# Encoder layer on one core: the first FFN product with 512-column matmuls, its partial products chained in three PSUM banks

## The reference, cut to what matters

```python
h = h + rmsnorm(mix, g_post_mix)
gu = rmsnorm(h, g_pre_ffn) @ w_ffn_in        # (512, 2048) @ (2048, 11264)
g, u = jnp.split(gu, 2, axis=-1)
h = h + rmsnorm((jax.nn.silu(g) * u) @ w_ffn_out, g_post_ffn)
```

## Time and profile before

| | us |
|---|---|
| median of 3 runs | 2728.7 (2728.43 to 2729.52) |
| the profiled execution, its own time | 2728.66 |
| its span, first to last instruction | 2726.5 |
| granted TensorE clock, mean | 0.998 |
| TensorE busy in matmuls | 2694.1 |
| VectorE busy | 1946.7 |
| ScalarE busy | 1086.7 |

### The profile page before, as it was taken

The page is one execution under the profiler, slowest core; times in us unless marked ns, Lnnn a source line. Parts: engine busy times, 40 slices in busy tenths (PEclk is TensorE's granted clock), DMA queues, the critical chain, the costliest instruction groups (busy, mean ns, idle before and its releaser), DMA issues.

```text
span 2726.5 us, 41873 instructions
## 1 busy us (share of the span) xinstructions
PE 2694.1 (99%) x16358; PEld 2416.1 (89%) x16358; DVE 1946.7 (71%) x2269; ACT 1086.7 (40%) x1413; POOL 338.1 (12%) x205
## 2 busy tenths in 40 slices
PE   8999999999999999999999999999999999999997
PEld 7999888888888888878999999999999888888886
DVE  7888655555554432276999999999998888886524
ACT  7333333333334422253444444444444444444422
POOL 0000000000000000000244344343433000000000
PEclk9999999999999999999999999999999999999999
DMA  6433522222225544253444434344346755544322
GB/s 257 155 117 117 150 91 77 77 82 88 77 89 152 148 152 146 94 187 121 171 144 146 154 142 167 133 155 164 123 173 258 259 187 183 214 167 153 139 93 108
DMA packets 174237, 396.15 MB, mean 145 GB/s; under 512 B 17846, under 2 KB 52014, under 8 KB 171566
## 3 DMA queue, kind: packets, MB, share of 16 engines
q1 hardware_dynamic: 149120, 340.99, 36.6%
q10 hardware_dynamic: 25006, 53.60, 5.1%
HBM read 336.81 MB, written 57.73 MB: 145 GB/s over the span
## 4 chain that ended last, share of the span: by engine, by line
PE 85%; issue 10%; DMA 1%; DVE 1%; ACT 1%; SPq 0%; POOL 0%; DVEq 0%; POOLq 0%
PE bank L2339 10%; PE bank L2337 10%; PE bank L2338 10%; PE bank L2178 8%; PE bank L2179 8%; PE bank L2180 8%; PE bank L2417 5%; PE bank L2418 5%; PE bank L2419 5%; PE bank L2586 4%; PE bank L2588 4%; PE bank L2589 4%; PE bank L2211 1%; DMA x_f<-xT 1%; DMA o_a_first<-w_ffn_pieces 0%
## 5 line engine op out<-in xcount | busy, mean ns | idle before, releaser
L2337 PE MATMUL bank<-act_hi,w_hi 128*128 128x256 f32 x1664 | 471.2, 283 | 2.4 <-DVE act_lo L1449 1.4
L2338 PE MATMUL bank<-act_lo,w_hi 128*128 128x256 f32 x1664 | 470.9, 283 | 0.0
L2339 PE MATMUL bank<-act_hi,w_lo 128*128 128x256 f32 x1664 | 470.9, 283 | 0.0
L844 ACT CAST w_hi<-w_raw 128x1024 fp32r<-128x1024 f32 x210 | 211.7, 1050 | 585.3 <-PE bank L2180 326.6
L1358 DVE TENSOR_TENSOR w_lo<-w_raw,w_hi 128x1024 fp32r<-128x1024 f32 x208 | 246.5, 1222 | 244.3 <-ACT w_hi L844 244.3
L2337 PEld LDWEIGHTS bank<-act_hi,w_hi 128*128 128x128 f32 x1664 | 319.4, 192 | 2.9 <-DVE act_lo L1449 1.6
L2338 PEld LDWEIGHTS bank<-act_lo,w_hi 128*128 128x128 f32 x1664 | 319.5, 192 | 0.1
L2339 PEld LDWEIGHTS bank<-act_hi,w_lo 128*128 128x128 f32 x1664 | 319.5, 192 | 0.0
L2178 PE MATMUL bank<-act_hi,w_hi 128*128 128x512 f32 x752 | 296.2, 394 | 0.3 <-DVE w_lo L1358 0.3
L2179 PE MATMUL bank<-act_lo,w_hi 128*128 128x512 f32 x752 | 293.1, 390 | 0.0
L2180 PE MATMUL bank<-act_hi,w_lo 128*128 128x512 f32 x752 | 293.0, 390 | 0.0
(11 more groups left out here) (293 smaller groups left out, 5952.5 us busy)
## 6 DMA issues: line engine op xcount, KB each, us to landing
w_raw<-w_in SPq DMA_DIRECT2D x92, 512.0 KB, 4.0
w_a_even<-w_ffn_in SPq DMA_DIRECT2D x80, 512.0 KB, 4.3
xop<-xop_dram SPq DMA_DIRECT2D x35, 1024.0 KB, 11.5
w_a_odd<-w_ffn_in SPq DMA_DIRECT2D x60, 512.0 KB, 4.7
xop_dram<-h_sums ACTq DMA_DIRECT2D x20, 1024.0 KB, 6.4
o_a_odd<-w_ffn_pieces SPq DMA_DIRECT2D x40, 512.0 KB, 7.7
o_a_even<-w_ffn_pieces SPq DMA_DIRECT2D x39, 512.0 KB, 6.9
w_raw<-w_ffn_in SPq DMA_DIRECT2D x36, 512.0 KB, 5.2
```

What stands on the lines that cost most here:

```text
L2337: nc.tensor.matmul(out, w_hi[:, slot, k], hi, start=k == 0, stop=False)
L2338: nc.tensor.matmul(out, w_hi[:, slot, k], lo, start=False, stop=False)
L2339: last = nc.tensor.matmul(out, w_lo[:, slot, k], hi, start=False, stop=k == HALF - 1)
```

## The change

- A product of the first FFN stage is 8 times two matmuls: the high weight against high and low activation side by side (512 columns, two runs of 256 in `act_both` for P0, P3, P5, P6, one run in `d1`, `t2`, `d2`), and the low weight against the high activation (256 columns, added to the first half of the same bank). The two halves of a bank are added when it is read.
- The products of a pair go into three banks: a takes P0 and P3, g takes P1 and P5, b takes a copy of P0, then P2, P4 and P6. Even pairs use banks 0, 1, 5, odd pairs 2, 3, 4.
- ScalarE makes six copies per pair (`keep_chain`) in place of one; before P2, P4 and P6 PE waits for one of them (`kept`).
- VectorE's additions become six, one pair's last ones at the start of the next pair (`finish_up`, `finish_hidden`). All four sums of weight blocks stay on VectorE; they move ahead of the low part of their step, and the fourth moves from step 6 to step 0 of the next pair (`ffn_fourth`).
- Silu, the high parts of the hidden tiles, GpSimd's low part of the sums and their stores move to later steps. The banks of the second product and of the tail are renumbered. The landing semaphores of `xop` are grouped as (0), (1, 2), (3, 4), (5, 6) in place of (0, 1), (2, 3), (4, 5), (6).

The core of the diff:

```diff
+PAIR_BANKS = ((0, 1, 5), (2, 3, 4))
+PAIR_CHAIN = (0, 1, 2, 0, 2, 1, 2)
-CHAINS = (((2, 3), (4, 5), (6, 7)), ((0, 1), (4, 5), (2, 3)), ((6, 7), (4, 5), (0, 1)))
+CHAINS = (((0, 1), (2, 5), (6, 7)), ((3, 4), (2, 5), (0, 1)), ((6, 7), (2, 5), (3, 4)))
...
-        xop_landed = [sem(f"xop_landed{j}") for j in (0, 2, 4, 6)]
+        xop_landed = [sem(f"xop_landed{j}") for j in (0, 1, 3, 5)]
...
             def operands(i, first=False):
+                if not first:
+                    low_of_sums(i + (-1))
                 pool.wait_ge(hid_ready, i * 2 + (CH + 1))
...
-                pool.wait_ge(h_summed, i * SUMS + SUMS)
-                pool.wait_ge(h_hi_ready, i * 3 + 3)
-                low_in_place(h_sums, slice(0, 4))
...
+            def keep_chain(n, q, j, first):
+                a, g, b = PAIR_BANKS[q % 2]
+                if j == 0:
+                    if not first:
+                        act.wait_ge(combined, n * COPIES + (COMBINED_FFN - COPIES))
+                    nc.scalar.copy(bank[:, b], bank[:, a]).then_inc(kept, 1)
+                elif j == 1:
+                    if not first:
+                        act.wait_ge(combined, n * COPIES + (COMBINED_FFN - COPIES + 2))
+                    nc.scalar.copy(second_kept[:].rearrange("p a t -> p (a t)"), bank[:, g]).then_inc(kept, 1)
+                elif j == 2:
+                    if not first:
+                        act.wait_ge(combined, n * COPIES + (COMBINED_FFN - COPIES + 5))
+                    nc.scalar.copy(third_kept[:].rearrange("p a t -> p (a t)"), bank[:, b]).then_inc(kept, 1)
+                elif j == 3:
+                    act.wait_ge(combined, n * COPIES + COMBINED_FFN)
+                    nc.scalar.copy(low_half[:], bank[:, a, S:]).then_inc(kept, 1)
+                elif j == 4:
+                    act.wait_ge(hid_ready, n + CH)
+                    nc.scalar.copy(up_kept[:].rearrange("p a t -> p (a t)"), bank[:, b]).then_inc(kept, 1)
+                elif j == 6:
+                    act.wait_ge(combined, n * COPIES + (COMBINED_FFN + 1))
+                    nc.scalar.copy(low_half[:], bank[:, b, S:]).then_inc(kept, 1)
...
                         act.wait_ge(op_done, p * PRODUCTS + (GATE_PAIRS * PRODUCTS + j + 1))
-                        if j == 0:
-                            nc.scalar.copy(first_product[:], bank[:, 0, 0:S]).then_inc(first_kept, 1)
+                        keep_chain(p, q, j, first and (q == 0 or j == 0 and q == 1))
...
+                        if j == 0:
+                            open_gate(f + (-1))
+                        if j == 2:
+                            high_of_hidden(f + (-1), q % 2 == 0)
+                        if q % 2 == 0 and j == 5:
+                            high_of_sums(r, q // 2)
+                        if q % 2 and j == 1 and not (first and q == 1):
                             store_sums(r, q // 2, r * 2 + (q // 2 - 1))
-                        if j == 3 and q % 2:
+                        if q % 2 and j == 5:
                             act.wait_ge(h_lo_ready, r * 6 + (1 + 3 * (q // 2)))
                             store_operands(r * 2 + q // 2, h_even, 1, 0, 0)
...
                     for j in range(PRODUCTS):
+                        if j == 0 and before:
+                            ffn_fourth(n, q % 2)
+                            finish_up(n + (-1), (q + 3) % 4)
+                        if j == 1 and before:
+                            if q % 2:
+                                finish_hidden(n + (-1), q - 1, None if first and q == 1 else r * 32 + 16 * (q // 2), h_even,
+                                              r * (2 * SUMS) + SUMS * (q // 2))
+                            else:
+                                finish_hidden(n + (-1), q + 3, None if first else r * 64 + 32 * (q // 2 - 1), h_odd, None)
                         if j == 4:
+                            dve.wait_ge(kept, n * COPIES + 4)
+                            combine(gu[:, 0], low_half[:], bank[:, a, 0:S])
+                        if j == 5:
+                            dve.wait_ge(kept, n * COPIES + 5)
+                            combine(both(up_kept), both(up_kept), both(second_kept))
+                        if j == 6:
+                            dve.wait_ge(op_done, n * PRODUCTS + (COMBINED_FFN + 6))
+                            combined_before(2)
+                            combine(up_kept[:, 1], up_kept[:, 0], up_kept[:, 1])
+                            combine(both(third_kept), both(third_kept), bank[:, g])
                             combined_before(4)
+                            combine(gu[:, 1], third_kept[:, 0], third_kept[:, 1])
+                            combined_before(5)
+                            nc.vector.tensor_tensor(both(gu), both(gu), rstd[:], ALU.mult).then_inc(ffn_read, 1)
+                        if 2 <= j <= 4 and not (last and q == 3):
+                            ffn_sum(n + 1, q + 1, j - 1)
...
+            def chained_product(n, q, j):
+                pe.wait_ge(lo_ready, n * PRODUCTS + (COMBINED_FFN + H_SEVEN + j + 3))
+                slot = (H_SEVEN + COMBINED_FFN + PRODUCTS * q + j) % 4
+                out = bank[:, PAIR_BANKS[q % 2][PAIR_CHAIN[j]]]
+                for k in range(HALF):
+                    parts = both_parts(j, k)
+                    nc.tensor.matmul(out.rearrange("p (a t) -> p a t", a=2), w_hi[:, slot, k], parts,
+                                     start=j < 2 and k == 0, stop=False, skip_group_check=True)
+                    last = nc.tensor.matmul(out[:, 0:S], w_lo[:, slot, k], parts[:, 0], start=False,
+                                            stop=k == HALF - 1, skip_group_check=True)
+                last.then_inc(op_done, 1)
+
+            def chain_free(n, j, first):
+                if j == 0 and not first:
+                    pe.wait_ge(combined, n * COPIES + (COMBINED_FFN - 2 * COPIES + 1))
+                if j == 1 and not first:
+                    pe.wait_ge(combined, n * COPIES + (COMBINED_FFN - 2 * COPIES + 4))
+                if j in (2, 4, 6):
+                    pe.wait_ge(kept, n * COPIES + (j - 1))
```

More of the change, by code:

```diff
@@ L469, in build @@
         out_four = sem("out_four")
+        kept = sem("kept")
         out_read = sem("out_read")
@@ L2088, in add_block @@
             def add_block(fb, t):
-                src = bank[:, 4 * (fb % 2) + t]
+                src = bank[:, TAIL_BANKS[fb][t]]
                 if fb < 2:
```

218 lines of the change are left out of this document (138 added, 80 removed).

## The result

The changed kernel takes **2721.3 us** (median of 8 runs, 2719.5 to 2724.0), the kernel before 2728.9 (8 runs on the same chip). The ratio is 0.9972, interval 0.9961 to 0.9983: faster, by 7.6 us where 24 were forecast. The profiled execution has 2719.83 us of its own and a span of 2717.7 (before 2728.66 and 2726.5), so the two traces differ by 8.8 us where the medians differ by 7.6.

A forecast was written before the change was run, and what follows sets the result against it. TensorE's matmuls, covering 2694.1 of 2726.5 us, were taken as the bound, with VectorE 95% busy. 2728.66 - 29.9 (TensorE) + 0.5 (change of stage) + 40 x 0.13 (VectorE) = 2704.5 us; range 2697 to 2722.

The forecast's parts named there:

- TensorE's part: First FFN stage: 512 plus 256 columns take 0.3467 us per input tile, down from 0.3600; 29.9 us less over 40 pairs.
- a change of width costs nothing extra: TensorE's stream: going from 512 to 256 columns keeps the 0.23 us distance seen in the attention, so nothing is added.
- VectorE's part: First FFN stage: VectorE needs 19.54 us per pair, just over TensorE's 19.41; 0.13 us per pair added.
- the same 2.8 us of stretch: VectorE's operations slowed beside GpSimd's: 2.8 us per pair, as before, since GpSimd's work is the same.
- rival 1: First FFN stage: VectorE is stretched more, up to 0.5 us per pair, 20 us more, up to 2724.5 us; chance 0.23.
- ScalarE's part: First FFN stage: ScalarE gains 2.7 us per pair, 11.8 of 19.41; TensorE's waits for its copies cost nothing.
- The change of stage: From first to second product: TensorE waits some 3.5 us in place of 1.06; no gain, and 0.5 us lost.
- the first wait goes: Change of stage: landings grouped to ask for operand 0 alone remove TensorE's 2.01 us wait for the second operand.
- x: Change of stage: the time by which VectorE is late, said to move it all by as much.
- Rival 2: TensorE's stream: each run of 256 columns keeps its fixed 0.0133 us, so merging saves nothing; at most 2728.7 us; chance 0.07.
- Rival 3: First FFN stage: later stores hold ScalarE; slower, 2739 us at a landing of 13 us, 2799 at 16; chance 0.13.
- What would show it: Signs for the trace: right, 512-column starts 0.347 us apart, pairs of 19.4 to 19.6 us; wrong, pairs over 19.7 us.

The follow-up runs named there:

- half_low_part: Changed kernel with TensorE leaving out the low part of the weights for k tiles 4 to 7 of each product; 2714.8 us.
- twelve_more_512: Changed kernel with the first 512-column matmul of a pair issued twice, 12 times in all; 2722.4 us, ratio 0.9973.
- late_up_sum: Changed kernel with VectorE's addition inside `up_kept` moved behind the multiplication `gu` times rstd; 2719.2 us, ratio 0.9963.
- short_fourth_sum: Changed kernel with the fourth sum of weight blocks made over one eighth of its width; 2718.3 us.
- split_256: Changed kernel with each 512-column matmul cut into two of 256 columns into the halves of the same bank; 2734.4 us.
- all_three_early: Changed kernel with 12 doubled 512-column matmuls, VectorE's `up_kept` addition behind the multiplication, and SP's first two operands ahead of its wait; 2708.6 us, ratio 0.9921.
- operands_first: Changed kernel with SP sending operands 0 and 1 of the second product before its wait for VectorE's low part; 2718.0 us, ratio 0.9959.
- all_three_each: Changed kernel with VectorE's addition moved, SP's two operands first, and a 512-column matmul doubled once every four pairs, 10 in all; 2709.0 us, ratio 0.9927.

## Why the prediction was wrong

The direction was right, the size was not: 7.6 us in place of 24. That the time lies inside the range of 2697 to 2722 us is luck. The range was that wide for a VectorE held up more, and the larger part of what is missing is a slow stream of TensorE, which no rival had.

**TensorE's part failed at the step "a change of width costs nothing extra".** It was read from one hand-over in the attention, rounded to 0.01 us, and a stream was priced by it. The kernel's stream runs in the slow rhythm, 353.3 and not 346.7 ns: 2240 x 6.67 ns = 14.9 us, the whole difference between 29.9 and 15.0. It is not a price per change of width either, since a quarter of the changes left it as it was. The price of 0.3467 us itself was not false, since it is what the same stream takes in its other rhythm. The step "no row shows a moving operand in two runs; I take zero" held. By the figure of 2.5 ns in the Trainium skill, TensorE: Matmul & The Clock Gate, section Back-to-back issue gap, the merged matmuls would have brought an estimated 5.6 us; they brought 15.0, and in the fast rhythm what 13.3 ns gives.

**VectorE's part was mis-sized by 0.31 us.** It needs 19.85 us per pair, not 19.54. The count of its work held; "the same 2.8 us of stretch" did not, it is 3.1. The upper bound named the right operations, additions out of SBUF alone, but gave each 0.54 us where one was locked out for 2.2. In the forecast VectorE was 0.13 over TensorE's pace; against the true 19.79 it is 0.06 over, which VectorE's lead covered for 33 pairs, and which cost some 0.7 us behind 1947 us, made up for by the fast tiles there. It is nevertheless a second cause: alone it holds the pairs at 19.85, and the stage at 787.2 us (`half_low_part`). Taking away either bound by itself won nothing in the stage (`twelve_more_512`, `late_up_sum`), both together won 11.3 us, and the stage came to 781.7, where the forecast had 808.0 - 29.9 + 5.2 = 783.3. (The prediction's 19.75 us for VectorE before should be 19.73, and its lower end 2698 should be 2697; nothing hangs on either.) This was rival 1, with 0.23, and its mechanism took part; its size in the stage could not show behind a slower TensorE.

**ScalarE's part** held: 57% busy where 61% were expected, and the profile lists no wait of TensorE for its copies. The two starts that are 0.1 us late (1947.3 and 1987.0) come right behind such a copy (1947.20 and 1986.86), and ahead of the copy ScalarE had itself stood 1.2 us for a sum of VectorE's.

**The change of stage failed at the step "the first wait goes".** Operand 0 was itself late, issued 5.6 us before the stage's last matmul and not 10.8 as before, since SP stood behind VectorE's low part of P5. The prediction had said that a VectorE late by x moves it all by x, and had taken x as zero; x is 5.2 us. It had 3.5 us of waits in one place, where five add up to 8.1. With VectorE relieved (`short_fourth_sum`) x falls to 1.8, and with the old stream (`split_256`), where VectorE keeps up, to 2.2. By this some 3 us of it are load and some 2 the new order. Most of the loss does not hang on x, though: both of these kernels still wait 5.4 and 5.5 us. In place of a loss of 0.5 us the change of stage cost 5.6 (6.1 less 0.5), with the start 0.5 later besides.

**Rival 2** (nothing saved) is out. **Rival 3**: GpSimd does wait for landed stores, up to 11.3 us, and nothing else waits for that; no slower kernel came of it.

What would show it had named the sign that came: "matmuls of 256 columns that start later than 0.2267 us after a 512-column one", and a pair over 19.7 us.

Of the second product one thing is closed and one open. If TensorE's waits inside it and the cost of half clock are taken out, it takes some 381 to 382 us in every run, the kernel before included; between 386.1 and 389.9 us stand the totals of the kernels with the changed code, apart from the one with the old landing groups, which has its wait ahead. So nothing but waits and clock is lost there. Open is which part of the change makes the waits. The longest, 2.6 us for VectorE's copies out of a chain's banks, stands in most versions and was 1.1 before; neither the order of the last pair's additions and pieces nor the renumbered banks of the second product were tried by themselves. What in TensorE makes the two rhythms is open too; only their entry and loss were seen.

## What to carry to other kernels

Price a new mixture of instructions by rows of that mixture, or keep both ends: a single hand-over does not tell how a stream settles. When two engines stand within a per cent of each other, an edit to either shows nothing; take both away at once before calling one of them harmless. Where an engine slightly slower than the other starts with a lead, look at the end of the stage for the first wait. And where a queue waits for one engine's progress, put the transfers that do not need it ahead of that wait.

## Not expected of the hardware

- TensorE streams 512 and 256 columns in turn in two stable rhythms, 353.3 and 346.6 ns per tile of both. Two 512s in a row on the tile with the 241 ns distance lead to the fast one; on the tile with 236 ns they do not. Two matmuls of 256 for one of 512 lead back. Behind a late start the stream goes on in either. In `all_three_early` the fast one held from 1324 us to the end of the stage, through nearly 740 us with a doubled matmul every 78 us.
- 512 and 128 columns in turn take 340 ns once settled, where their columns and 13.3 ns each make 293. All 384 columns stand 173.5 apart, at the price.
- VectorE's addition with both inputs in SBUF is held to the end of a GpSimd operation already running (2.62 for 0.41 us, 1.91 for 0.42); with one input in PSUM it is not (0.67 us).
- After 2.6 us without a matmul TensorE was granted 1.2 GHz for 3.4 us (`operands_first`), and after 2.2 us as well (`all_three_early`); the changed kernel had stood 2.66 us before 2106.05 and `all_three_each` 2.23 before 2094.87, and both were granted 1.00 behind it. The length of the wait alone does not tell which comes.
